# Retention and pooling trunk on one Trainium2 core: half of the chunks of h transposed by DMA instead of by TensorE

## The reference, cut to what matters

```python
h = x                                            # 256 x 2048, two layers
h = h + retention_branch(rms_norm(h, ret_norm), ret_w_in, ret_w_out)        # layer 0
h = h + sigmoid(rms_norm(h, ple_norm[0]) @ ple_w_gate[0]) * (p[0] @ ple_w_proj[0])
h = h + pool_branch(rms_norm(h, pool_norm), pool_w_in, pool_w_group, scale, pool_w_out)  # layer 1
h = h + sigmoid(rms_norm(h, ple_norm[1]) @ ple_w_gate[1]) * (p[1] @ ple_w_proj[1])
out = rms_norm(h, final_norm)
```

## Time and profile before

| | |
|---|---|
| time, median of 3 runs | 1565.87 us (1565.81 to 1565.88) |
| the profiled execution's own time | 1565.69 us |
| its span from first to last instruction | 1563.9 us |
| mean granted TensorE clock | 0.997 of full speed |
| busy: PE, DVE, ACT | 1550.4, 1019.8, 843.6 us |
| DMA transposes issued (two a turn) | 56 |

### The profile page before, as it was taken

The page is one execution under the profiler, slowest core; times in us unless marked ns, Lnnn a source line. Parts: engine busy times, 40 slices in busy tenths (PEclk is TensorE's granted clock), DMA queues, the critical chain, the costliest instruction groups (busy, mean ns, idle before and its releaser), DMA issues.

```text
span 1563.9 us, 18979 instructions
## 1 busy us (share of the span) xinstructions
PE 1550.4 (99%) x6938; PEld 1283.1 (82%) x6938; DVE 1019.8 (65%) x1247; ACT 843.6 (54%) x1000; POOL 4.6 (0%) x12
## 2 busy tenths in 40 slices
PE   9999999999999999999999999999999999999997
PEld 6888888888888888888888888888888888888885
DVE  6766666666666666667656585775577557755665
ACT  6455554635555463555645556654664476445553
POOL 0000000000000000000000000000000000000000
PEclk9999999999999999999999999999999999999998
DMA  9575555647556654755455666755765576554551
GB/s 375 220 228 188 190 201 188 215 163 239 188 175 210 202 194 181 224 185 193 158 197 189 192 230 199 241 188 193 225 212 203 188 215 225 212 206 172 180 193 75
DMA packets 102583, 314.73 MB, mean 201 GB/s; under 512 B 63968, under 2 KB 63984, under 8 KB 66960
## 3 DMA queue, kind: packets, MB, share of 16 engines
q1 hardware_dynamic: 101408, 310.14, 58.2%
q0 software_dynamic: 704, 3.27, 0.6%
q10 hardware_dynamic: 432, 0.79, 0.2%
HBM read 297.40 MB, written 2.10 MB: 192 GB/s over the span
## 4 chain that ended last, share of the span: by engine, by line
PE 98%; DVE 1%; DMA 0%; ACT 0%; issue 0%; SPq 0%; DVEq 0%; ACTq 0%
PE accA L376 12%; PE accA L377 12%; PE accA L378 12%; PE accC L376 11%; PE accC L377 11%; PE accC L378 11%; PE accB L376 8%; PE accB L378 8%; PE accB L377 8%; PE side L392 1%; DMA w_raw<-in_stream_dram 0%; PE side L431 0%; PE side L430 0%; PE side L429 0%; PE side L420 0%; PE side L421 0%
## 5 line engine op out<-in xcount | busy, mean ns | idle before, releaser
L959 DVE TENSOR_TENSOR w_lo<-w_raw,w_hi 128x1024 fp32r<-128x1024 f32 x551 | 667.7, 1223 | 405.7 <-ACT w_hi L637 403.6
L637 ACT CAST w_hi<-w_raw 128x1024 fp32r<-128x1024 f32 x551 | 575.9, 1053 | 547.4 <-PE accA L378 207.7
L376 PE MATMUL accC<-w_hi,xa_hi 128*128 128x512 f32 x512 | 199.4, 389 | 0.5 <-DVE w_lo L959 0.5
L377 PE MATMUL accC<-w_lo,xa_hi 128*128 128x512 f32 x512 | 199.2, 389 | 0.0
L378 PE MATMUL accC<-w_hi,xa_lo 128*128 128x512 f32 x512 | 199.2, 389 | 0.0
L376 PE MATMUL accA<-w_hi,xa_hi 128*128 128x512 f32 x508 | 197.7, 389 | 0.0
L378 PE MATMUL accA<-w_hi,xa_lo 128*128 128x512 f32 x508 | 197.6, 389 | 0.0
L377 PE MATMUL accA<-w_lo,xa_hi 128*128 128x512 f32 x508 | 197.6, 389 | 0.0
L376 PEld LDWEIGHTS accC<-w_hi,xa_hi 128*128 128x128 f32 x512 | 96.1, 188 | 20.9 <-DVE w_lo L959 1.0
L378 PEld LDWEIGHTS accC<-w_hi,xa_lo 128*128 128x128 f32 x512 | 96.1, 188 | 20.0
L377 PEld LDWEIGHTS accC<-w_lo,xa_hi 128*128 128x128 f32 x512 | 96.1, 188 | 19.8
(11 more groups left out here) (209 smaller groups left out, 2183.4 us busy)
## 6 DMA issues: line engine op xcount, KB each, us to landing
w_raw<-in_stream_dram SPq DMA_DIRECT2D x275, 1024.0 KB, 4.8
h<-in_x_dram SPq DMA_DIRECT2D x4, 512.0 KB, 13.8
xT_raw<-in_xT_dram SPq DMA_DIRECT2D x3, 512.0 KB, 15.3
dec<-in_decay_dram POOLq DMA_DIRECT2D x1, 1024.0 KB, 9.0
fgain<-in_final_gain_dram POOLq DMA_DIRECT2D x1, 1024.0 KB, 6.6
out_dram<-emb SPq DMA_DIRECT2D x1, 1024.0 KB, 3.8
halvesT<-halves SPq DMA_TRANSPOSE x56, 5.3
w_raw<-in_stream_dram SPq DMA_DIRECT2D x2, 256.0 KB, 6.4
```

The lines of the kernel that those rows point to most:

```text
L376: pe.matmul(acc[pair][t][:, 0:n], xh, wh, start=first and b == 0, stop=False)
L377: pe.matmul(acc[pair][t][:, 0:n], xh, wl, start=False, stop=False)
L637: act.copy(w_hi[:, r % RING, :], w_raw[:, r // 2, (r % 2) * 1024:(r % 2 + 1) * 1024]).then_inc(hi_ready, 1)
L959: dve.tensor_tensor(w_lo[:, r % RING, :], w_raw[:, r // 2, (r % 2) * 1024:(r % 2 + 1) * 1024], w_hi[:, r % RING, :].bitcast(F32), ALU.subt ...
```

## The change

Six of the twelve chunks, c = 0 to 2 of stages 2 and 3, get a turn. The chunks of stage 1 and the last chunk of stages 2 and 3 (`BY_PE`) stay with PE. `H_TURNS` gives the unit behind whose split ACT parts a chunk: units 23, 31 and 39 of the first close for stage 2, units 10, 14 and 18 of the second close for stage 3. `JOIN` gives how many units later ACT joins it: 5 in stage 2, 4 in stage 3. SP's places are ten units behind the parting, rounded down to an even unit: 32, 40 and 48 for stage 2, and 20, 24 and 28 for stage 3. The buffers lie in memory that is idle then (`in_close`). The two small memsets of `sums` move from the first close to unit 4 of the first group. New names of the buffers: `halves_r`, `halvesT_r`, `words_r` in stage 2, `_p` in stage 3, `_e` for those that were there.

```diff
@@ -82,6 +82,15 @@
 U_LATER = (2 * KD_U - 2, 3 * KD_U - 2)
 LANDING = 7
 TURNS = 2 * (HEADS - 1)
+Z0 = EMB_U + NC * RO_U
+H_TURNS = (tuple((2, c, Z0 + KD_U * (c + 1) + 3) for c in range(NC - 1)),
+           tuple((3, c, EMB_U + PO_U * (c + 1) + 2) for c in range(NC - 1)))
+BY_PE = [(1, c) for c in range(0, NC)] + [(2, NC - 1), (3, NC - 1)]
+JOIN = (None, 4, 5, 4)
+AHEAD = 10
+LATE = Z0 + KD_U * (NC - 1) + 3 + JOIN[2] - (Z0 + GATE_U)
+POOL_TURNS = TURNS + len(H_TURNS[0])
+CLOSE_TURNS = POOL_TURNS + 4 * GROUPS - 2
...
+        half_oT = KG // 2 * SEQ * 4
+        in_close = (turn_buffers("_r", oT0 + half_oT, oT0 + KG * SEQ * 4 + half_oT, arena0 + 32 * 1024),
+                    turn_buffers("_p", arena0 + 40 * 1024, arena0 + 44 * 1024, sig0))
...
-            def pieces(u0, u1, loop, n, turns):
+            def pieces(u0, u1, loop, n, turns, bufs):
 
                 for q in range(u0 // 2, u1 // 2):
                     for j, u in enumerate(turns):
                         if u == 2 * q - u0:
                             sp.wait_ge(halves_ready, n + (2 * j + 2))
                             sp.sem_inc(turn_begun, 1)
-                            transpose_halves()
+                            transpose_halves(bufs[j])
                     next_round(loop + q // RAW, q % RAW)
...
-            pieces(CLOSE_A, POOL0, 0, 0, ())
-            pieces(POOL0, POOL1, 0, 2 * TURNS, (20, 28))
+            turns = [at_u + AHEAD - at_u % 2 for _stage, _c, at_u in H_TURNS[0]]
+            pieces(CLOSE_A, POOL0, 0, 2 * TURNS, turns[:-1], [in_close[0]] * len(turns[:-1]))
+            pieces(POOL0, POOL1, 0, 2 * POOL_TURNS - 2, (turns[-1] - (POOL0 - CLOSE_A), 20, 28), [in_close[0], in_emb, in_emb])
...
-            pieces(CLOSE_B, UNITS, 0, 0, ())
+            turns = [at_u + AHEAD - at_u % 2 for _stage, _c, at_u in H_TURNS[1]]
+            pieces(CLOSE_B, UNITS, 0, 2 * CLOSE_TURNS, turns, [in_close[1]] * 3)
...
                     for cc in range(NC):
-                        if u == EMB_U + ou * (cc + 1):
+                        if u == EMB_U + ou * (cc + 1) and (2 * layer + 1, cc) in BY_PE:
                             h_transposes(2 * layer + 1, cc)
-                        if cc < NC - 1 and layer == 0 and u == EMB_U + NC * ou + KD_U * (cc + 1) + 1:
-                            h_transposes(2, cc)
...
+            def h_halves(stage, c):
+                act.wait_ge(h_ready, NC * (stage - 1) + c + 1)
+                halves_of(h[:, :, c * COL:(c + 1) * COL], in_close[stage // 3])
+
+            def h_words(stage, c, turn):
+                bufs = in_close[stage // 3]
+                if stage > 1 and c:
+                    act.wait_ge(xT_ready, NC * (stage - 1) + c)
+                words_of(turn, bufs, bufs[2])
+                act.wait_ge(words_ready, turn * 2 + 2)
+                stream_hi(stage, c)
...
-                        if u == z + 4 and layer == 0:
-                            stream_hi(2, c)
+                    for i, (stage, c, at_u) in enumerate(H_TURNS[layer]):
+                        if u == at_u + JOIN[stage]:
+                            h_words(stage, c, turn0 + i)
+                        if u == at_u:
+                            h_halves(stage, c)
...
-                        if u == z + 4 and layer == 0:
-                            stream_lo(2, c)
+                    for stage, c, at_u in H_TURNS[layer]:
+                        if u == at_u + JOIN[stage]:
+                            stream_lo(stage, c)
```

More of the change, by code:

```diff
@@ L137, in trunk, with turn_buffers @@
         emb = sb("emb", [P, TT, D], F32)
-        halves = nc.alloc_sbuf_tensor_at("halves", [P, TT, 2, COL], U16, offset=emb0)
-        halvesT = nc.alloc_sbuf_tensor_at("halvesT", [P, 2 * COL // P, SEQ], U16, offset=emb0 + 4096)
-        words = nc.alloc_sbuf_tensor_at("words", [P, COL // P, SEQ], F32, offset=emb0 + 8192)
+        def turn_buffers(name, a, b, c):
+            return (nc.alloc_sbuf_tensor_at("halves" + name, [P, TT, 2, COL], U16, offset=a),
+                    nc.alloc_sbuf_tensor_at("halvesT" + name, [P, 2 * COL // P, SEQ], U16, offset=b),
+                    nc.alloc_sbuf_tensor_at("words" + name, [P, COL // P, SEQ], F32, offset=c))
+        in_emb = turn_buffers("_e", emb0, emb0 + 4096, emb0 + 8192)
+        words = in_emb[2]
         pT_hi = sb("pT_hi", [P, 2, KP, SEQ], F32R)
         pT_lo = sb("pT_lo", [P, 2, KP, SEQ], F32R)
+        sig0 = nc.sbuf_base
         sig = sb("sig", [P, TT, COL], F32)
@@ L398, in h_transposes @@
                 pe.wait_ge(h_ready, NC * (stage - 1) + c + 1)
-                if stage + c > 1:
-                    pe.wait_ge(xT_ready, NC * (stage - 1) + c)
+                if stage == 1 and c > 0:
+                    pe.wait_ge(xT_ready, c)
+                if stage == 2:
+                    pe.wait_ge(xT_ready, NC)
                 transpose4(lambda t: h[:, t, :], c * COL).then_inc(hT_done, 1)
@@ L655, in stream_hi @@
                 hi = xb_hi if stage % 2 else xa_hi
-                act.wait_ge(hT_done, NC * (stage - 1) + c + 1)
+                if (stage, c) in BY_PE:
+                    act.wait_ge(hT_done, BY_PE.index((stage, c)) + 1)
                 for j in range(4):
                     k = 4 * c + j
-                    cp = act.activation(hi[:, k, :], side[j // 2][:, (j % 2) * SEQ:(j % 2 + 1) * SEQ], ACT.Copy,
-                                        scale=gain[:, stage, k:k + 1])
+                    src = side[j // 2][:, (j % 2) * SEQ:(j % 2 + 1) * SEQ]
+                    if (stage, c) not in BY_PE:
+                        src = in_close[stage // 3][2][:, j, :]
+                    cp = act.activation(hi[:, k, :], src, ACT.Copy, scale=gain[:, stage, k:k + 1])
                     if j % 2:
@@ L683, in pr_hi_part, with halves_of, words_of @@
                 act.copy(pr_hi[:], pr[:]).then_inc(pr_hi_ready, 1)
-            def halves_of(src):
+            def halves_of(src, bufs):
                 for t in range(TT):
-                    act.copy(halves[:, t, :, :], src[:, t, :].bitcast(U16).rearrange("p (n two) -> p two n", two=2)
+                    act.copy(bufs[0][:, t, :, :], src[:, t, :].bitcast(U16).rearrange("p (n two) -> p two n", two=2)
                              ).then_inc(halves_ready, 1)
-            def words_of(n, dst):
+            def words_of(n, bufs, dst):
                 act.wait_ge(halvesT_landed, n * (16 * TT) + 16 * TT)
@@ L710, in y_halves @@
                 act.wait_ge(y_gated, hd + 1)
-                halves_of(yn)
+                halves_of(yn, in_emb)
             def y_words(hd):
                 act.wait_ge(qkT_ready, hd + 1)
-                words_of(hd * 2, words)
+                words_of(hd * 2, in_emb, words)
                 act.wait_ge(words_ready, hd * 4 + 2)
@@ L767, in uT_part @@
                     act.wait_ge(d_scaled, n)
[L768 removed]
+                words_of(turn, in_emb, uT)
             def m_halves(n, c):
                 act.wait_ge(m_ready, n + 1)
[L772 removed]
+                halves_of(gm[:, c, :, :], in_emb)
             def m_words(n, k0, c, turn):
@@ L776, in m_words @@
                     act.wait_ge(mT_ready, n)
-                words_of(turn, words)
+                words_of(turn, in_emb, words)
                 act.wait_ge(words_ready, turn * 2 + 2)
@@ L839, in group @@
                 n2 = g * 2
-                turn = TURNS if first else TURNS - 2 + g * 4
+                turn = POOL_TURNS if first else POOL_TURNS - 2 + g * 4
                 turns = U_FIRST if first else U_LATER
@@ L846, in group @@
                         finished(2 * NC - 1, 2)
+                    if first and u == LATE:
+                        h_words(2, NC - 2, POOL_TURNS - 1)
                     if first and u == 4:
@@ L997, in stream_lo @@
                         dve.wait_ge(hT_hi, 2 * (NC * (stage - 1) + c) + j // 2 + 1)
+                    src = side[j // 2][:, (j % 2) * SEQ:(j % 2 + 1) * SEQ]
+                    if (stage, c) not in BY_PE:
+                        src = in_close[stage // 3][2][:, j, :]
                     ins = dve.scalar_tensor_tensor(
-                        out=lo[:, k, :], in0=side[j // 2][:, (j % 2) * SEQ:(j % 2 + 1) * SEQ],
+                        out=lo[:, k, :], in0=src,
                         scalar=gain[:, stage, k:k + 1], in1=hi[:, k, :].bitcast(F32), op0=ALU.mult, op1=ALU.subtract)
@@ L1217, in group @@
                         add_gated(NC - 1)
+                    if first and u == LATE:
+                        stream_lo(2, NC - 2)
                     if first and u == 4:
@@ L1220, in group @@
                         row_scale(2)
+                        dve.wait_ge(xT_ready, 2 * NC)
+                        for b in sums:
+                            own.mark(dve.memset(b[:, :, 0:PAD], 0.0))
                     if not first and u == 2:
@@ L1275, in close @@
                             ins.then_inc(h_ready, 1)
-                        if u == e + 3:
```

(1 more changed line is left out.)

27 lines of the change are left out of this document (14 added, 13 removed).

## The result

The changed kernel takes 1574.97 us (median of 6 runs, 1573.83 to 1575.36), the kernel before 1565.88 us (1565.81 to 1565.94) beside it. The ratio is 1.0057, with a 95% interval from 1.0047 to 1.0067. The prediction was 1574.7 us, so sign and size came as worked out. The profiled execution took 1575.09 us, with a span of 1573.3 us, and its mean granted clock was 0.994 of full speed.

The account below looks back on a forecast made before the run. The prediction took PE's work to bound the kernel, busy 1550.4 of 1563.9 us. It summed 1565.7 - 5.2 + 13.2 + 1.0 = 1574.7 us, slower by 0.6%, with an 8 in 10 range of 1571.5 to 1580.8.

Parts of the forecast that it names:

- Its signs: New PE waits for `w_lo` and ACT waits for landings in the second close, transposes behind a piece, 48 fewer on L415.
- the third wait of PE: Second close, chunk 2, `w_lo` 19 to 23: 15.1 us against 11.8 us of PE work, so PE waits 3.3 us.
- The gain, 5.2 us: Six chunks of 8 transposes leave PE, 0.87 us each on the chain: 5.2 us, all on the path.
- SP's place holds the transposes back: SP issues the transposes only behind the piece ahead in its list, which waits for a later unit's `w_lo`.
- its 8.5 us: Time taken from `w_lo` to the landing of the transposes in both closes, with bounds 8.1 and 9.7 us.
- The first wait, 3.8 us: Second close, unit 15: `w_lo` ready at 1452.4, PE wants it at 1448.6, so PE waits 3.8 us.
- The second, 6.1 us: Second close, chunk 1, `w_lo` 15 to 19: 17.0 us against 10.9 us of PE work, so PE waits 6.1 us.
- All three waits are longer: Each PE wait in the second close exceeds the 2.3 us of idleness that took the clock from 2.4 to 1.2 GHz.
- the heavy rival: Half clock behind the last wait in the second close is paid, 2.7 us: 1577.4 us, 1583.4 with slow landings; chance 0.12.
- The sum in the second close: PE's three waits in the second close together: 13.2 us, 12.0 to 16.8 by the bounds for landing.
- The first close, 1.0 us: Stage 2: late landings cost 0.5 us for each of two turns, 1.0 us together, bounds 0.2 and 3.4.
- Loads run ahead: Pieces are loaded some seven units ahead, so they aren't late for PE and cost nothing.

Follow-up runs that it names:

- stage 2 alone: The changed kernel with the chunks of stage 3 left on PE, so only the first close is changed: 1564.48 us, ratio 0.9992 to the kernel before.

## Why the prediction was right, step by step

Its signs came: the waits of ACT for the three landings (4.3, 8.0 and 6.5 us), the transposes 0.4 to 0.5 us behind a piece and 2.7 us after the parting, 48 transposes fewer on L415. The one that did not is the third wait of PE. Three figures of its working are 0.1 us off by rounding (1566.8, 1572.8 and the first wait's 1452.4); nothing hangs on them.

- **The gain, 5.2 us.** Right: twice as many transposes cost 5.2 us, and with the waits gone the change gains 5.4.
- **SP's place holds the transposes back.** Right, and shown from both sides: one piece earlier 14.7 us less, one piece later 10.6 more. The place works in two ways, by what the piece ahead waits for and by that piece being in flight; the prediction had both in its 8.5 us, and the traces give the second the larger share.
- **The first wait, 3.8 us.** It was 3.2. Landing came 8.0 us behind the `w_lo`, where I took 8.5 and, by the rows, 8.1 as the lower bound.
- **The second, 6.1 us.** From `w_lo` to `w_lo` it took 17.95 us where I had 17.0, since this landing came 9.5 us behind, near the upper bound. PE had 10.9 us of work, so unit 19 came 7.1 us later by this joint: 5.6 us idle and 1.5 of half clock in unit 15.
- **The third, 3.3 us of waiting.** The time was nearly right and the picture wrong. From unit 19 to unit 23 it took 14.56 us (15.1 predicted) less 11.7 of work, 2.8 us. But 2.7 of these are half clock and 0.1 idle. The failed sentence is "All three waits are longer": I had said that half clock is taken from the next wait, and did not take it from the third, which by that has 0.6 us left. This is also why the heavy rival did not come: with no third wait there is no half clock behind it. In the kernel with the later places, where the third wait is real, it came, and my expectation for that kernel was too low.
- **The sum in the second close.** 3.2 + 7.1 + 2.8 = 13.1 us against 13.2. That it is so close is in part luck: the second landing's 1.0 us more made up for the other two.
- **The first close, 1.0 us.** Three ways to read it give 1.2 to 1.6. In the profile the first `u` of the pooling layer comes at 860.45 where it was at 861.89, 1.44 us earlier with 2.6 gained, so 1.2 lost; stage 2 alone shows 1.35; with its places earlier 1.56 come back. The size was right and the picture wrong: I had given 0.5 us to each of two turns, and it is one wait, behind the first of them.

```profile
801.91 0.50 PE L399 MATMUL accB<-w_hi,xb_hi 128*128 128x512 f32 x1 [0.86 <-DVE w_lo L1003]
```

The landing of the first turn came 9.6 us behind its `w_lo` (17.0 us behind the sigmoid's start, where I had 15.9), that of the second 8.0 (15.5), and PE didn't wait behind that one. By starts of matmuls the one wait cost 1.25 us. That the sum came out is luck here too.

- **Loads run ahead.** Right: in neither close does the view of waits show an engine that waited for a piece (`w_raw`).

In the span: -5.2 + 13.1 + 1.2 = 9.1 us, where 9.4 were measured. Most of the 0.3 us left lies at 1504.57 and 1504.93, where two matmuls start 0.36 and 0.35 us before their next instead of 0.23: PE's weight load waits there once more for a `w_lo` (0.4 us).

## What to carry to other kernels

A DMA queue that is written as a list is an engine of its own: before you ask how long a transfer takes, ask what the entry ahead of it waits for. Put a transfer ahead of the entry that waits for something produced later than its data, and leave no large load in flight before it. When a chain of waits is set by another engine, as here, what TensorE loses at half clock between two of them is free; only what follows the last is paid.

## What the runs showed of the hardware

- A pair of DMA transposes of 128x1024 16-bit numbers landed in 2.8 us in stage 3 without a load in flight (one of the first close took 4.4), in 6.2 to 7.8 behind one piece of 1 MB, in 6.9 to 8.3 behind two. Issuing it held SP for 2.6 us in the first case, for 5.5 and 6.1 to 6.3 in the others, nearly all of the difference in the second of the two (1.3 us alone, 4.2 behind a piece).
- Landings behind one piece at the same distance differed by 1.5 us (8.0 and 9.5 us behind the `w_lo` in stage 3, 8.0 and 9.6 in stage 2). The runs don't say why.
- A wait of 3.2 us, in which PE started nothing, was enough for the clock to fall from its upper to its lower level: the last window without a matmul shows 0.92, the next 0.50. The Trainium skill (TensorE: Matmul & The Clock Gate, Part 1) has idleness bring the clock down, and the trace agrees. The half clock cost 1.5 us behind the first wait and 2.7 us, a whole unit, behind the second. The length of the wait alone doesn't settle it: with the second wait filled, the clock stayed up through a wait of 3.0 us before unit 15 and fell in one of 2.5 us before unit 23.
